# Delta rule: the next pair's squares, row sums and decay rows placed ahead of this pair's output norm and turn

## The chip, the cores and the metric

One core of a Trainium2 chip. The metric is the device time of one execution in microseconds; the kernel before takes 4389.96 us (median of 3 runs, 4386.17 to 4395.65).

## The reference, cut to what matters

The kernel is one inference step of a decoder layer: a projection, a gated delta rule beside sparse attention, an output projection and a convolutional feed-forward network, for 2048 prompt tokens and 8 sample tokens. The change touches the delta rule over the prompt (4 heads of 128, processed in chunks). For each chunk and head:

```python
q = l2_normalize(q) * (GDN_DK ** -0.5)      # needs the row sums of q*q
k = l2_normalize(k)                         # needs the row sums of k*k
gc = jnp.cumsum(g, axis=-1)
diff = gc[..., :, None] - gc[..., None, :]
decay = jnp.where(lower, jnp.exp(jnp.where(lower, diff, 0.0)), 0.0)
a_mat = jnp.where(strict, jnp.einsum('bhnid,bhnjd->bhnij', k * beta[..., None], k) * decay, 0.0)
sol = triangular_solve(a_mat + eye, [v * beta, k * beta * exp(gc)])
...
def step(s, xs):                            # from chunk to chunk
    v_new = u_c - w_c @ s
    o = q_c @ s + qk_c @ v_new
    s = s * gl_c + k_c.T @ v_new
    return s, o
...
o = rms_norm(o, out_gain) * jax.nn.silu(z)  # needs the row sums of o*o
```

## The kernel before, in words

`build` runs phases one after the other, each closed by a barrier: projection, channels, `heads`, mix, feed-forward up and down. `heads` has two parts. The second, named "mid", runs the delta rule (`Delta`) with attention heads of 8 query tiles (`Attention`, the tiles in `LATE`) beside it.

**Tiling.** The prompt is 16 chunks of 128 tokens, taken in 8 pairs `j`; `b` is 0 or 1 in a pair, `n = 2j + b`. Four heads lie side by side, so that most tiles are 128 x 512 fp32. Each chunk `b` has two PSUM tiles of one bank, `A[b]` and `B[b]`; the other four banks belong to the attention.

**Order.** Each engine has a written order of instructions (methods `tensor`, `scalar`, `gpsimd`, `vector`, `sync` of `Delta`), tied together by semaphores in `S`. In each pair, on TensorE: row sums of the squares (L1893, each matmul against ones, 64 columns); decay rows (L1902); key turn (L1908), value turn (L1915), normalised keys turned back (L1921), Gram products (L1930), system turned (L1937); six levels of the block inverse (L1949, L1957, L1959); then `W` (L1966), new values (L1975, L1976), state update product (L1981) and outputs (L1985, L1986), the last four chunk by chunk, since chunk 1 needs the state of chunk 0; last the normed outputs turned (L1996).

ScalarE squares q and k (L2009), takes exponentials of the decays (L2013, L2020, L2021), the root of the key and query sums (L2016), copies PSUM tiles out (L2027, L2033, L2039, L2045, L2050), squares the output (L2053), and takes the root for the output norm (L2056). VectorE reads the sums (L2121), forms the decay differences (L2128 to L2130), scales the keys (L2133, L2136), applies the decays (L2152, L2155), updates the inverse (L2164 to L2179), updates the state (L2188), reduces the output squares (L2194 to L2198), scales the output (L2201, L2203) and gates it (L2209). GpSimd spreads the gates (L2072), forms the two scaled keys (L2079, L2080), masks decays (L2085) and scales queries (L2087). SyncE loads q, k, v and z, and stores the result.

**Attention beside.** `Beside` is a generator of attention steps. After each piece of the delta rule an engine calls `side.spend(w)`, with a weight `W_...` of that piece. It issues attention steps until the share of the attention's total weight (248.0) that is issued reaches the share of the rule's total (833.6) that is spent, 0.2975 to 1. All engines spend the same weights in the same order, so each sees the same attention step at the same place. On TensorE a step is a score product (L1603 with L1605 or L1607), or four blocks turned (L1618) and the weighting of the blocks before (L1654). On ScalarE it is the eviction of a score (L1680) or of turned blocks (L1689), or a head's exponential (L1694), with square roots for the query norm at L1724. On VectorE it is a head's bias and maximum (L1770, L1771), for which the exponential waits.

Of the kernel before, what the change touches and what calls it, by code (L numbers as in the profile page):

```python
# [1456 lines left out]
class Attention:  # L1457
# [32 lines left out]
    def rows(self, t):  # L1490

        return slice(self.tiles[t] * P, self.tiles[t] * P + P)
# [309 lines left out]
class Delta:  # L1802
# [47 lines left out]
    def sync(self, sp, side, pairs, ahead):  # L1850
        S, N = self.S, self.N
        if 0 in pairs:
            sp.dma_start(self.gain[:, :], self.out_gain).then_inc(S["gain"], 16)
        for j in pairs:
            side.spend(2 * (self.W_SUMS + self.W_ROWS + self.W_TURN_K + self.W_TURN_V + self.W_BACK + self.W_GRAM))
            if j == 0:
                for b in range(2):
                    self.load_z(sp, b)
# [5 lines left out]
            for w in (self.W_SYS, *[self.W_YV + self.W_PROD] * (LEVELS - 1), self.W_WT, self.W_VNEW, self.W_KVO, self.W_NORM):  # L1864
                side.spend(2 * w)
            for b in range(2):
# [17 lines left out]
    def tensor(self, pe, side, pairs):  # L1884
        K, S, A, B = self.K, self.S, self.A, self.B
        for j in pairs:
            for b in range(2):
                n = j * 2 + b
                pe.wait_ge(S["sq"], n + 1)
                if j:  # L1890
                    pe.wait_ge(S["on"], n - 1)
                for i in range(2 * GH):
                    last = pe.matmul(self.sums_in(B[b])[:, i, :], self.kwd[b][:, i, :], K.ones[:, 0:64], start=True, stop=True)  # L1893
                last.then_inc(S["ss"], 1)
                side.spend(self.W_SUMS)
# [73 lines left out]
            for b in range(2):  # L1969
# [31 lines left out]
    def scalar(self, act, side, pairs):  # L2001
        S, A, B, st = self.S, self.A, self.B, self.st
        for j in pairs:
            for b in range(2):
# [5 lines left out]
                side.spend(self.W_SUMS)  # L2010
            for b in range(2):
                act.wait_ge(S["dif"], j * 2 + b + 1)
                act.activation(self.er[b][:, :, :], A[b][:, :, :], ACT.Exp).then_inc(S["er"], 1)  # L2013
                if b == 1:
                    act.wait_ge(S["sums"], j * 2 + 2)
                    act.activation(st[:, :, 8:12], st[:, :, 4:8], ACT.Sqrt).then_inc(S["root"], 1)  # L2016
                side.spend(self.W_ROWS)
            for b in range(2):
# [28 lines left out]
            for b in range(2):  # L2047
# [5 lines left out]
                act.activation(self.kwd[b][:, 0:GH, :], B[b][:, :, :], ACT.Square).then_inc(S["osq"], 1)  # L2053
# [1237 lines left out]
```

## Time and profile before

| | us |
|---|---|
| median of 3 runs | 4389.96 |
| the profiled execution's own time | 4385.17 |
| its span, first to last instruction | 4383.7 |
| TensorE busy in the span | 3860.7 (88%) |
| VectorE busy | 2198.2 (50%) |
| ScalarE busy | 1552.3 (35%) |
| GpSimd busy | 651.7 (15%) |
| mean granted TensorE clock | 0.928 |

The time of an execution is its span and a little around it (1.5 us here). The page and the views give busy times by engine, by stretch and by line; a line is that of the kernel's source. Idle time of an engine counts only where the engine sets the pace. The granted clock is 1 at 2.4 GHz and 0.5 at 1.2 GHz; a stretch's mean lies between.

### The profile page before, as it was taken

To read this page: it belongs to the slowest core of one execution; us is meant where nothing else is said; L and a number is where in the kernel's file an instruction comes from. 1 tells how busy PE (TensorE), PEld (TensorE's weight loads), DVE (VectorE), ACT (ScalarE), POOL (GpSimd) and SP (SyncE) were. 2 spreads that over 40 slices of the span, in tenths; PEclk is the share of its full clock that TensorE was granted. 3 is DMA by queue.
4 is the path that set the end of the run, shared out by engine and by line. 5 is a ranking of instruction groups with operands and counts; after the bars stand their busy time and mean duration, and the time that the engine had idled before them with its cause. 6 is when DMAs were issued, how large, how long until landed. Compare 5 with 4: busy or idle time off the path is not lost. (4 is left out here: it accounts for less than half of the span.)

```text
span 4383.7 us, 51967 instructions
## 1 busy us (share of the span) xinstructions
PE 3860.7 (88%) x19810; PEld 3155.5 (72%) x19882; DVE 2198.2 (50%) x4366; ACT 1552.3 (35%) x2462; POOL 651.7 (15%) x530
## 2 busy tenths in 40 slices
PE   7998887788859877888888779899999999979999
PEld 4554454455448556777777778799999999958787
DVE  6648988998953583343433343443444444330200
ACT  2135565565636333333433331322222222221211
POOL 0000000000000003222322220011111111024443
PEclk9998999999979677999988889999999999989999
DMA  3342212120141201111111114311211112064433
GB/s 111 96 97 62 67 41 78 37 65 25 54 172 64 68 12 56 28 35 34 32 33 33 44 51 129 102 39 39 58 39 47 49 39 58 29 206 135 130 117 109
DMA packets 287498, 298.52 MB, mean 68 GB/s; under 512 B 33871, under 2 KB 231375, under 8 KB 282410
## 3 DMA queue, kind: packets, MB, share of 16 engines
q1 hardware_dynamic: 264254, 249.46, 20.0%
q10 hardware_dynamic: 20944, 25.59, 1.7%
q0 software_dynamic: 2112, 20.97, 1.3%
q8 instruction: 117, 1.92, 0.2%
q14 instruction: 71, 0.58, 0.0%
HBM read 202.15 MB, written 94.10 MB: 68 GB/s over the span
## 5 line engine op out<-in xcount | busy, mean ns | idle before, releaser
L538 PE MATMUL chan_p_g<-ht,w_chan 128*128 128x412 f32 (+1 forms) x1760 | 677.3, 528 | 53.4 <-ACT chan_flat L586 33.7
L949 PE MATMUL up_p_g<-ht_high,up_wh 128*128 128x412 f32 (+1 forms) x1760 | 617.2, 351 | 0.2 <-POOL up_wl L1006 0.2
L949 PE MATMUL up_p_g<-ht_low,up_wh 128*128 128x412 f32 (+1 forms) x1760 | 615.3, 350 | 0.0
L949 PE MATMUL up_p_g<-ht_high,up_wl 128*128 128x412 f32 (+1 forms) x1760 | 615.0, 349 | 0.0
L538 PEld LDWEIGHTS chan_p_g<-ht,w_chan 128*128 128x128 f32 x1760 | 341.3, 197 | 300.6 <-issue 233.4
L970 ACT ACTIVATE up_pre<-up_p_g 128x412 f32<-128x412 f32 (+1 forms) x220 | 113.2, 515 | 738.1 <-PE up_p_g L949 738.1
L1348 ACT ACTIVATE chan_signed<-chan_sc,chan_trial 128x512 bf16<-128x512 f32 (+6 forms) x224 | 304.9, 1361 | 148.5 <-DVE chan_trial L1403 127.8
L1038 DVE TENSOR_SCALAR up_acc<-up_pre,up_taps 128x2048 f32<-128x2048 f32 x44 | 59.3, 1347 | 557.4 <-ACT up_pre L970 557.4
L949 PEld LDWEIGHTS up_p_g<-ht_high,up_wh 128*128 128x128 f32 x1760 | 331.5, 188 | 1.8 <-POOL up_wl L1006 0.6
L949 PEld LDWEIGHTS up_p_g<-ht_low,up_wh 128*128 128x128 f32 x1760 | 331.3, 188 | 1.2
L949 PEld LDWEIGHTS up_p_g<-ht_high,up_wl 128*128 128x128 f32 x1760 | 331.2, 188 | 0.5
L1389 DVE TENSOR_SCALAR_CACHE_REDUCE chan_tie<-chan_sc,chan_trial 128x384 bf16<-128x384 f32 (+6 forms) x224 | 316.3, 1412 | 7.6
L1006 POOL TENSOR_TENSOR up_wl<-up_w,up_wh 128x1024 fp32r<-128x1024 f32 x44 | 131.3, 2984 | 1085.3 <-ACT up_wh L964 826.5
L1324 PE MATMUL chan_p_sc<-ik,chan_iq 128*128 128x512 f32 (+3 forms) x304 | 187.0, 619 | 101.5 <-ACT chan_r L1343 91.1
L1206 PE MATMUL down_p_y<-down_wl,down_ah 128*128 128x512 f32 x704 | 274.4, 390 | 0.0
L1205 PE MATMUL down_p_y<-down_wh,down_ah 128*128 128x512 f32 x704 | 274.3, 390 | 0.0
L1207 PE MATMUL down_p_y<-down_wh,down_al 128*128 128x512 f32 x704 | 274.2, 389 | 0.0
L1177 POOL TENSOR_TENSOR down_al<-down_a,down_ah 128x1024 fp32r<-128x1024 f32 x88 | 211.8, 2406 | 356.9 <-ACT down_ah L1151 356.9
L1343 ACT ACTIVATE chan_r<-chan_p_sc 128x512 f32<-128x512 f32 (+3 forms) x304 | 159.6, 543 | 222.5 <-PE chan_p_sc L1325 116.2
L1151 ACT ACTIVATE down_ah<-down_a 128x1024 fp32r<-128x1024 f32 x88 | 93.3, 1060 | 382.3 <-PE down_p_y L1207 374.3
L1222 DVE TENSOR_TENSOR down_x<-down_p_y,down_x 128x512 f32<-128x512 f32 (+1 forms) x34 | 21.1, 680 | 388.0 <-PE down_p_y L1207 388.0
L1375 DVE SCALAR_TENSOR_TENSOR chan_sc<-chan_r,chan_iw,chan_sc 128x512 f32<-128x512 f32 (+3 forms) x266 | 172.6, 683 | 54.1 <-ACT chan_r L1343 51.7
(561 smaller groups left out, 7033.9 us busy)
## 6 DMA issues: line engine op xcount, KB each, us to landing
down_a<-scratch_act SPq DMA_DIRECT2D x88, 512.0 KB, 3.7
scratch_act<-up_acc SPq DMA_DIRECT2D x22, 1028.0 KB
up_w<-in_w_up SPq DMA_DIRECT2D x44, 512.0 KB, 6.4
chan_iq<-scratch_iq SPq DMA_DIRECT2D x28, 512.0 KB, 7.2
scratch_qkv<-chan_acc SPq DMA_DIRECT2D x12, 1028.0 KB, 4.6
keys_of_raw<-scratch_qkv SPq DMA_DIRECT2D x16, 768.0 KB, 5.4
w_chan<-in_w_in SPq DMA_DIRECT2D x22, 512.0 KB, 4.5
proj_x<-in_x_prompt SPq DMA_DIRECT2D x16, 512.0 KB, 3.9
```

The source lines that it names most:

```text
L538: last = pe.matmul(p_g[u % BANKS][:, 0:cols.stop - cols.start], weights[:, k, :], K.ht[:, k, cols], start=(k == 0), stop=(k == KD - 1))
L949: last = pe.matmul(p_g[u][:, 0:cols.stop - cols.start], wp[s][:, k, :], hp[:, k, cols], start=(k == 0 and m == 0), stop=(k == KD - 1 and m ...
L1006: pool.tensor_tensor(wl[s][:, :, :], w[s][:, :, :], wh[s][:, :, :].bitcast(F32), ALU.subtract).then_inc(s_wl[s], 1)
L1177: pool.tensor_tensor(al[t % RING][:, :, :], a[t % RING][:, :, :], ah[t % RING][:, :, :].bitcast(F32), ALU.subtract)\
L1205: pe.matmul(bank[0:m, :], hi, wh[:, f, :], start=(f == 0), stop=False)
L1206: pe.matmul(bank[0:m, :], hi, wl[:, f, :], start=False, stop=False)
L1207: last = pe.matmul(bank[0:m, :], lo, wh[:, f, :], start=False, stop=(f == NF - 1))
L1324: pe.matmul(out, self.iq[b][:, 0, h, :], self.K.ik2[:, cols], start=True, stop=False)
L1343: act.activation(self.r[n % self.RING][:, 0:width], self.p_sc[n % 2][:, 0:width], ACT.Relu).then_inc(S["relu"], 1)
L1348: act.activation(self.signed[:, 0:nk], self.sc[1][:, 0:nk], ACT.Sign, scale=-1.0, bias=self.trial[:, 1:2].bitcast(F32), accum_out=self.sig ...
L1375: dve.scalar_tensor_tensor(out=s[:, cols], in0=r, scalar=w, in1=s[:, cols], op0=ALU.mult, op1=ALU.add)\
L1389: last = dve.tensor_scalar(self.tie[:, 0:na], self.sc[0][:, 0:na], trial[:, 0:1].bitcast(F32), None, ALU.is_ge, ALU.add, accum_out=count[: ...
```

## The change

For pairs 1 to 7 the first three steps of a pair move ahead of the output norm, gate and turn of the pair before. To make room in PSUM, the sums go to `A[b]` instead of `B[b]`, the outputs are turned into `B[b]` instead of `A[b]`, and the output squares go to a free tile of the inverse (`y[1]`) instead of `kwd`, which then holds the next pair's squares. The waits follow. The root of the key and query sums now stands ahead of the exponentials and right behind the root of the output norm. The weights are spent in the new order on every engine.

```diff
@@ sync
+        side.spend(2 * (self.W_SUMS + self.W_ROWS))
+        for b in range(2):
+            self.load_z(sp, b)
         for j in pairs:
-            side.spend(2 * (self.W_SUMS + self.W_ROWS + self.W_TURN_K + self.W_TURN_V + self.W_BACK + self.W_GRAM))
-            if j == 0:
-                for b in range(2):
-                    self.load_z(sp, b)
+            side.spend(2 * (self.W_TURN_K + self.W_TURN_V + self.W_BACK + self.W_GRAM))
...
+            if j + 1 < N // 2:
+                side.spend(2 * (self.W_SUMS + self.W_ROWS))
+            side.spend(2 * self.W_NORM)
@@ tensor
-        for j in pairs:
+
+        def begin(j):
             for b in range(2):
                 n = j * 2 + b
                 pe.wait_ge(S["sq"], n + 1)
                 if j:
-                    pe.wait_ge(S["on"], n - 1)
+                    pe.wait_ge(S["state"], n - 1)
                 for i in range(2 * GH):
-                    last = pe.matmul(self.sums_in(B[b])[:, i, :], self.kwd[b][:, i, :], K.ones[:, 0:64], start=True, stop=True)
+                    last = pe.matmul(self.sums_in(A[b])[:, i, :], self.kwd[b][:, i, :], K.ones[:, 0:64], start=True, stop=True)
                 last.then_inc(S["ss"], 1)
                 side.spend(self.W_SUMS)
             for b in range(2):
                 n = j * 2 + b
                 pe.wait_ge(S["gb"], n + 1)
-                if j:
-                    pe.wait_ge(S["res"], n - 1)
+                pe.wait_ge(S["sums"], n + 1)
                 for h in range(GH):
                     last = pe.matmul(A[b][:, h, :], self.el[b][:, h, :], K.upto[:, :], start=True, stop=True)
                 last.then_inc(S["row"], 1)
                 side.spend(self.W_ROWS)
-            for b in range(2):
-                pe.wait_ge(S["sums"], j * 2 + b + 1)
+        begin(pairs[0])
+        for j in pairs:
+            for b in range(2):
+                if j:
+                    pe.wait_ge(S["res"], j * 2 + b - 1)
                 for h in range(GH):
                     last = pe.matmul(B[b][:, h, :], self.raw[b][:, GH + h, :], K.ident[:, :], start=True, stop=True)
                 last.then_inc(S["turnk"], 1)
@@ tensor, after the outputs
+            if j + 1 < self.N // 2:
+                begin(j + 1)
             side.spend(self.W_NORM)
             side.spend(self.W_NORM)
             for b in range(2):
                 n = j * 2 + b
                 pe.wait_ge(S["on"], n + 1)
-                pe.wait_ge(S["state"], n + 1)
                 for h in range(GH):
-                    last = pe.matmul(A[b][:, h, :], self.kn[b][:, h, :], K.ident[:, :], start=True, stop=True)
+                    last = pe.matmul(B[b][:, h, :], self.kn[b][:, h, :], K.ident[:, :], start=True, stop=True)
@@ scalar: begin(j), called as on TensorE, after the output squares
                 act.activation(self.kwd[b][:, :, :], self.raw[b][:, 0:2 * GH, :], ACT.Square).then_inc(S["sq"], 1)
                 side.spend(self.W_SUMS)
+            if j:
+                act.wait_ge(S["mean"], j)
+                act.activation(st[:, :, 20:24], st[:, :, 16:20], ACT.Sqrt).then_inc(S["oroot"], 1)
+            act.wait_ge(S["sums"], j * 2 + 2)
+            act.activation(st[:, :, 8:12], st[:, :, 4:8], ACT.Sqrt).then_inc(S["root"], 1)
             for b in range(2):
                 act.wait_ge(S["dif"], j * 2 + b + 1)
                 act.activation(self.er[b][:, :, :], A[b][:, :, :], ACT.Exp).then_inc(S["er"], 1)
-                if b == 1:
-                    act.wait_ge(S["sums"], j * 2 + 2)
-                    act.activation(st[:, :, 8:12], st[:, :, 4:8], ACT.Sqrt).then_inc(S["root"], 1)
                 side.spend(self.W_ROWS)
...
-                act.activation(self.kwd[b][:, 0:GH, :], B[b][:, :, :], ACT.Square).then_inc(S["osq"], 1)
+                act.activation(self.y[1][b][:, :, :], B[b][:, :, :], ACT.Square).then_inc(S["osq"], 1)
@@ gpsimd: begin(j) holds the copy of L2072 and its weights, called after the weights of KVO
@@ vector
+        def sums(j):
+            if j:
+                dve.wait_ge(S["mean"], j)
             for b in range(2):
                 dve.wait_ge(S["ss"], j * 2 + b + 1)
-                dve.tensor_scalar(st[:, b, 0:8], self.sums_in(B[b])[:, :, 0], EPS, None, ALU.add).then_inc(S["sums"], 1)
+                dve.tensor_scalar(st[:, b, 0:8], self.sums_in(A[b])[:, :, 0], EPS, None, ALU.add).then_inc(S["sums"], 1)
                 side.spend(self.W_SUMS)
+
+        def rows(j):
             for b in range(2):
                 n = j * 2 + b
                 dve.wait_ge(S["row"], n + 1)
...
             dve.tensor_tensor(st[:, :, 16:20], st[:, :, 16:20], st[:, :, 0:4], ALU.add).then_inc(S["mean"], 1)
-            side.spend(self.W_NORM)
+            if j + 1 < self.N // 2:
+                sums(j + 1)
             dve.wait_ge(S["oroot"], j + 1)
             step(dve.reciprocal(st[:, :, 16:20], st[:, :, 20:24]))
             for b in range(2):
                 dve.tensor_tensor(self.kn[b][:, :, :], B[b][:, :, :], self.col(st[:, b, 16:20]), ALU.mult).then_inc(S["on"], 1)
+            if j + 1 < self.N // 2:
+                rows(j + 1)
+            side.spend(self.W_NORM)
             side.spend(self.W_NORM)
```

## Rows read from the trace of the kernel before

**Rows 1.** Stretches, mid phase: window, its us, each engine's busy us (instructions), clock, DMA

```profile
1747.00:2612.00 865.00, 723.80 (x5208) 664.41 (x5248) 325.07 (x738) 313.70 (x551) 240.19 (x281) 0.91 0.12 33
```

**Rows 2.** Same view, columns as above: the seven stretches between pairs, and their sum

```profile
1849.20:1889.90 40.70, 30.46 (x214) 28.23 (x213) 22.09 (x48) 17.77 (x29) 12.36 (x12) 0.92 0.31 83
1947.70:1988.60 40.90, 29.08 (x167) 23.48 (x169) 22.09 (x48) 20.31 (x31) 13.96 (x13) 0.92 0.24 65
2059.40:2097.90 38.50, 28.06 (x219) 25.89 (x217) 22.15 (x48) 17.62 (x28) 12.27 (x12) 1.00 0.32 89
2156.50:2196.80 40.30, 31.42 (x183) 25.75 (x183) 22.08 (x48) 20.51 (x30) 13.64 (x13) 0.92 0.25 65
2261.30:2309.60 48.30, 34.07 (x216) 31.36 (x214) 21.94 (x48) 17.39 (x26) 10.48 (x10) 0.86 0.26 71
2370.90:2416.30 45.40, 35.04 (x185) 29.11 (x186) 22.09 (x48) 19.66 (x28) 10.49 (x10) 0.81 0.22 58
2488.60:2536.30 47.70, 34.35 (x222) 31.15 (x221) 23.33 (x51) 19.72 (x30) 12.20 (x12) 0.85 0.21 66
sum 301.80, PE 222.48 PEld 194.98 DVE 155.78 ACT 132.97 POOL 85.41; mean PE 31.78 PEld 27.85 DVE 22.25 ACT 19.00 POOL 12.20
```

**Rows 3.** Waits, 1745 to 2615: waiter <- releaser: us in total, times, longest

```profile
PE mid_p_A L1949 <- DVE mid_xt L2168: 36.9, 16, 6.1
...
PE mid_p_B L1893 <- ACT mid_kwd L2009: 29.3, 10, 5.7
...
PE mid_p_A L1996 <- DVE mid_kn L2203: 18.9, 7, 3.2
...
PE mid_p_A L1930 <- ACT keys_of_raw L2027: 10.0, 6, 2.8
```

**Rows 4.** Groups, ScalarE, same stretch: table loads, count, busy us and mean ns

```profile
L1724 ACT ACT_TABLE_LOAD x8 | 10.3, 1283 | 0.1
L2016 ACT ACT_TABLE_LOAD x8 | 10.3, 1283 | 0.1
...
L2056 ACT ACT_TABLE_LOAD x4 | 5.1, 1283 | 0.1
```

**Rows 5.** Order of time, 2045 to 2085: start, us, instruction, [idle before <- releaser]

```profile
2055.47 1.02 PE L1603 MATMUL mid_p_a_l<-keys_of_kt,mid_a_qg 128*128 128x512 f32 x2
...
2059.43 0.60 ACT L2053 ACTIVATE mid_kwd<-mid_p_B 128x512 f32<-128x512 f32 x1 [1.99 <-PE mid_p_B L1986]
...
2062.66 1.29 DVE L2203 TENSOR_TENSOR mid_kn<-mid_p_B,mid_st 128x512 f32<-128x512 f32 x2
...
2063.41 1.16 PE L1996 MATMUL mid_p_A<-ident,mid_kn 128*128 128x128 f32 x8 [2.69 <-DVE mid_kn L2203]
...
2064.60 0.75 DVE L2209 SCALAR_TENSOR_TENSOR mid_x<-mid_p_A,mid_gain,mid_z 128x512 f32<-128x512 f32 x1 [0.66 <-PE mid_p_A L1996]
...
2065.52 1.04 ACT L2009 ACTIVATE mid_kwd<-keys_of_raw 128x1024 f32<-128x1024 f32 x1
...
2066.62 2.00 PE L1893 MATMUL mid_p_B<-ones,mid_kwd 128*128 128x64 f32 x16 [0.61 <-ACT mid_kwd L2009]
...
2072.09 1.11 PE L1902 MATMUL mid_p_A<-upto,mid_el 128*128 128x128 f32 x8
...
2073.24 0.69 DVE L2128 TENSOR_TENSOR mid_et<-mid_p_A,gc 128x512 f32<-128x512 f32 x1 [0.78 <-PE mid_p_A L1902]
...
2073.97 0.43 DVE L2129 TENSOR_SCALAR mid_el<-mid_et 128x512 f32<-128x512 f32 x1
...
2081.19 0.20 DVE L2133 RECIPROCAL mid_st<-mid_st 128x8 f32<-128x8 f32 x1 [2.43 <-ACT mid_st L2016]
...
2083.20 1.04 POOL L2080 TENSOR_TENSOR mid_kwd<-mid_kn,kdec 128x512 f32<-128x512 f32 x1
```

**Rows 6.** Order of time, VectorE, 2371 to 2416: maximum of an attention head

```profile
2379.82 2.29 DVE L1771 TENSOR_REDUCE mid_a_bias<-mid_a_lg 128x1 f32<-128x2048 f32 x1
```

**Rows 7.** Order of time, ScalarE, same stretch: the exponential behind that maximum

```profile
2382.14 2.00 ACT L1694 ACTIVATE mid_a_lg<-mid_a_lg,mid_a_bias 128x2048 f32<-128x2048 f32 x1 [6.08 <-DVE mid_a_bias L1771]
```

More of the change, by code:

```diff
@@ L2002, in scalar, with begin @@
         S, A, B, st = self.S, self.A, self.B, self.st
-        for j in pairs:
+        def begin(j):
             for b in range(2):
@@ L2013, in scalar @@
                 act.activation(self.er[b][:, :, :], A[b][:, :, :], ACT.Exp).then_inc(S["er"], 1)
-                if b == 1:
-                    act.wait_ge(S["sums"], j * 2 + 2)
-                    act.activation(st[:, :, 8:12], st[:, :, 4:8], ACT.Sqrt).then_inc(S["root"], 1)
                 side.spend(self.W_ROWS)
+        begin(pairs[0])
+        for j in pairs:
             for b in range(2):
@@ L2052, in scalar @@
                 act.wait_ge(S["kvo"], n + 1)
-                act.activation(self.kwd[b][:, 0:GH, :], B[b][:, :, :], ACT.Square).then_inc(S["osq"], 1)
+                act.activation(self.y[1][b][:, :, :], B[b][:, :, :], ACT.Square).then_inc(S["osq"], 1)
                 side.spend(self.W_KVO)
-            act.wait_ge(S["mean"], j + 1)
-            act.activation(st[:, :, 20:24], st[:, :, 16:20], ACT.Sqrt).then_inc(S["oroot"], 1)
+            if j + 1 < self.N // 2:
+                begin(j + 1)
+            else:
+                act.wait_ge(S["mean"], j + 1)
+                act.activation(st[:, :, 20:24], st[:, :, 16:20], ACT.Sqrt).then_inc(S["oroot"], 1)
             side.spend(self.W_NORM)
@@ L2066, in gpsimd, with begin @@
             pool.memset(K.state[:, :, :], 0.0).then_inc(S["zero"], 1)
-        for j in pairs:
+        def begin(j):
             for b in range(2):
@@ L2075, in gpsimd @@
             side.spend(self.W_ROWS)
+        begin(pairs[0])
+        for j in pairs:
             for b in range(2):
@@ L2106, in gpsimd @@
                 side.spend(self.W_PROD)
-            for w in (self.W_WT, self.W_VNEW, self.W_KVO, self.W_NORM, self.W_OUT):
+            for w in (self.W_WT, self.W_VNEW, self.W_KVO):
+                side.spend(w)
+                side.spend(w)
+            if j + 1 < self.N // 2:
+                begin(j + 1)
+            for w in (self.W_NORM, self.W_OUT):
                 side.spend(w)
@@ L2131, in vector @@
                 side.spend(self.W_ROWS)
+        sums(pairs[0])
+        rows(pairs[0])
+        for j in pairs:
             dve.wait_ge(S["root"], j + 1)
@@ L2193, in vector @@
                 dve.wait_ge(S["osq"], j * 2 + b + 1)
-                last = dve.tensor_reduce(st[:, b, 16:20], self.kwd[b][:, 0:GH, :], AX.X, ALU.add)
+                last = dve.tensor_reduce(st[:, b, 16:20], self.y[1][b][:, :, :], AX.X, ALU.add)
             dve.tensor_scalar(st[:, :, 0:4], st[:, :, 0:4], EPS * HD, None, ALU.mult)
@@ L2208, in vector @@
                 dve.wait_ge(self.s_z[b], j * 16 + 16)
-                dve.scalar_tensor_tensor(out=self.x[b][:, :, :], in0=A[b][:, :, :], scalar=self.gain[:, 0:1], in1=self.z[b][:, :, :],
+                dve.scalar_tensor_tensor(out=self.x[b][:, :, :], in0=B[b][:, :, :], scalar=self.gain[:, 0:1], in1=self.z[b][:, :, :],
                                          op0=ALU.mult, op1=ALU.mult).then_inc(S["res"], 1)
```

5 lines of the change are left out of this document (3 added, 2 removed).

## The prediction, made before the changed kernel was run

> **What bounds the kernel now.** I read the busy time in stretches first. The delta rule's phase with its side attention fills 1747 to 2612 us [rows 1]. It is the only part that the diff touches; before and after it lie barriers, so what is saved there comes off the end whole. TensorE is busy 723.8 of these 865 us, no other engine over 326, and its clock is 0.91. So TensorE sets the pace, and a gain is idle time of TensorE or time at its low clock. Next I cut out the stretch from the last output matmul of one pair (L1986) to the first level matmul of the next (L1949), which I call a seam. There are seven, numbered 0 to 6 by the pair that ends [rows 2]. They last 301.8 us, with 222.5 busy, so 79.3 idle: 10.2, 11.8, 10.4, 8.9, 14.2, 10.4 and 13.4. Seam 2 alone has the full clock throughout, so its 28.06 us busy is what the work costs at full clock; 7 x 28.06 = 196.4, and the missing 26.1 us are the price of the low clock. A seam without idle and low clock would be 28 us; the seven average 43.1.
>
> Then I asked the list of waits what ends the idle [rows 3]. Three chains show. The output norm: TensorE waits for L2203 before it turns the outputs (18.9 us). The next pair's squares: it waits for L2009 (29.3 us in ten waits, the longest 5.7). The keys: L1930 waits 10.0 us for ScalarE. The wait of L1949 (36.9 us over all eight pairs) belongs to the first inverse step, which the change leaves alone. Last the activation tables: 39 loads in the phase, six groups between 8 and 4 each, 1.283 us apiece, three of them in [rows 4]. The list in order of time [rows 5] shows one seam as a chain: outputs scaled, turned, gated; only then the squares of the next pair.
>
> **The change, part by part.** Prices are per seam; all durations are from [rows 5] unless another group stands there.
>
> Removed, norm wait. The turn waited for the chain of reduce, root and scale (2.69 idle at L1996). Afterwards TensorE has the row sums (2.00 twice) and decay rows (1.11 twice) to do first, 6.2 us, and VectorE's chain behind the last sums (0.2 read, 0.2 reciprocal, 1.29 for both scalings) is 1.9 with latencies. The decay rows cover it. Price of this wait: nothing left.
>
> Left at the front. TensorE still has nothing until the first square: 0.60 for the output square L2053 (the size of the other full-tile evictions) and 1.04 for L2009, 1.65 us together. Seven times: 11.5 us. The second square stands in ScalarE's queue behind one attention step. By the kernel's own sharing rule (0.2975 side units for each main unit) that step is a score eviction in seams 0 and 4 and a transposed-block eviction in 2 and 6; in 1, 3, 5 none falls there. A score must first be made (L1603, 1.02), evicted (about 0.65), then 1.04 squared: TensorE idles about 1.8. After a transposed block it has a weighting of 1.0 to do: 0.65. Sum 2 x 1.8 + 2 x 0.65 = 4.9 us.
>
> Added, wait of the key turn (L1908) for the gated output (`res`). Behind it in TensorE's queue stand the value turn and everything else; nothing else of the pair can start. VectorE must take the second decay differences first (0.69 + 2 x 0.43 = 1.6), then gate (0.75). With two turns (L1996, 1.16 each, about 0.95 from start to start) and one side step on TensorE this is covered in seams 0 and 1. Where an attention maximum (L1770, L1771: 0.4 + 2.29, [rows 6]) falls into the chain, it isn't. The sharing rule puts it between the two gatings in seam 2, after the second differences in 3, 4 and 5, and between the differences in 6. VectorE is then free for gating 4.5 us after the second decay row (rows: 0.2 + 1.6 + 2.7), the gate is done at 5.35, and TensorE has 2.7 to 4.3 of work: idle 1.6, 1.1, 1.15; in seam 6 about 2.2, in seam 2 1.3. Sum 7.4 us. Bounds: 0, if side steps are longer than I count, and 4.9 a seam (34 us) if nothing covers the chain.
>
> Moved, key root. Both square roots now stand together, ahead of the exponentials, and the root of the key sums is ready before the decay rows. L2133 waited 2.43 for it behind two exponentials and a table load; that goes. The key scaling can follow the key turn at once, before the value turn, and about 3 us earlier against the rest. Counting the order of Exp and Sqrt on ScalarE, with the side steps, gives the 39 loads of the trace for the old order and 23 for the new. The 16 loads are 16 x 1.283 = 20.5 us of ScalarE, which is busy 313.7 of 865 us [rows 1]: alone worth nothing; they count where ScalarE delays kh (L2027) and with it L1930. There the maximum and exponential of the attention stay in the chain, so I keep all 10.0 us of L1930's wait [rows 3] as the remaining idle between key turn and Gram products. Bounds: 0 to 10.
>
> The Trainium skill (ScalarE: Activation LUTs, What ACT_TABLE_LOAD costs) puts a switch at 1283 ns plus a drain of 1380 ns. The load agrees; no drain stands in this trace, where a 2.43 us wait holds the load, the Sqrt and the end of an exponential; with a drain of that size it could not. By that page the root would come an estimated 1.38 us sooner still in each seam, 9.7 us in seven, and the sum would be 4336.
>
> Kept: L1949's first wait. 36.9 us over eight pairs [rows 3], 7/8 of it in the seams' pairs, half before the first chunk's matmul: 16.1 us.
>
> Without price: the swap of PSUM tiles A and B for sums and output turn, and the output squares into y[1], keep counts and shapes. TensorE's new wait for `state` before the sums ends with L2188's four operations right after L1986, within the 1.65. VectorE's wait for `mean` is for its own last small operation (at most 0.2, beside the sums). GpSimd's copy L2072 is early in either order. SyncE: gating comes 8 to 10 us later in the seam, so the stores and the loads of z do too; z is used one pair (about 100 us) later, and `ahead` is used after the phase. The z loads for pair 0 come earlier. Pair 0's root order: 0 to -1.3 us, taken as 0.
>
> Sum of idle after: 11.5 + 4.9 + 7.4 + 10.0 + 16.1 = 49.9, against 79.3: 29.4 saved.
>
> Clock. The loss of 26.1 us comes with idle: seams 0 to 3 (8.9 to 11.8 idle) were busy (30.46 + 29.08 + 28.06 + 31.42)/4 = 29.76, a loss of 1.7 each; seams 4 to 6 (10.4 to 14.2) were busy 34.07, 35.04 and 34.35, a loss of 6.4 each [rows 2]. In 4 to 6 an attention exponential that waits for VectorE (6.08 us, [rows 7]) stood before or between the squares. The new order has it behind them in every seam. So I take 1.7 for all seven: 11.9, 14.2 saved. Bounds: 0 and 26.1.
>
> Total 43.6 us. The profiled execution took 4385.2 (span 4383.7), so 4341.6; the median of the runs is 4.8 above it, so 4346.
>
> **The rivals.**
> *Clock stays.* The sums' 64-column matmuls stand together behind an idle front, and the seams, which hold these sums, have a clock of 0.81 to 0.92 but for one [rows 2]. Against it: the seams with short idle lose little. Then only the 29.4 come: 4361.
> *The next wait.* Keys are ready earlier, but GpSimd needs five operations of 1.04 from there to the first masked decay and three more for the second. I count 8.2 us against 10.7 of TensorE work. If the side steps there are short, 3 us a seam come back: 4346 + 21 = 4367.
> *Nothing comes.* TensorE's gaps only change place, because each fused step still waits for its partner; within 0.2% (about 9 us, what a measurement of this kernel can tell from no change): 4390.
> *Slower, by the order of VectorE's queue.* The output scaling now stands behind both sums, and gating behind both decay differences and a maximum. If TensorE's side steps cover none of it, each seam has 1.65 + 1.8 + 4.9 = 8.35 idle, 58.5 in all, with 26.1 kept: 84.6, above the 79.3 before, and with long idle in each seam all take the clock loss of seams 4 to 6 (7 x 6.4 = 44.8, 18.7 more): 4390 + 24 = 4414. It decides from 11.3 us idle a seam. Against it: by the sharing rule six of the seven seams have an attention step (L1603 is one, [rows 5]) between the last decay row and the last output turn.
> The Trainium skill (PSUM — Partial Sum Buffer, Engine vs sequencer instructions) says that the queues of ScalarE, VectorE and GpSimd are strictly first in, first out; by it this rival's 4414 is what an uncovered chain gives. The trace agrees: the squares L2009 waited behind an exponential.
>
> **How the numbers follow.** Forecast (4330 to 4358) 0.44, clock 0.23, next wait 0.18, nothing 0.08, slower 0.07. Faster by over 0.2% 0.85, the same 0.08, slower 0.07. Best case: idle terms three and four at 0 (17.4) and no clock loss (11.9): 4317; I cut at 4322. The upper end goes past the third case with 9 us of error, 4376; what lies outside is mostly the last two.
>
> **What would show it.** Right: seven seams of 36 to 38 us; 23 table loads; L1996 without a wait; no wait of L2133 for a root; waits of L1908 for L2209 of 1 to 2 us in seams 2 to 6; L1893's waits near 2 us each; clock in the seams 0.9 or more in all. Wrong: L1908 waiting 4 us or more (slower rival), L2152 waiting for L2085 (next wait), seams 4 to 6 still near 0.85 (clock), or a body between seams that grows by what the seam lost, which would mean that attention work was only shifted.

## The result, and the profile of the changed kernel

| | before | changed |
|---|---|---|
| median of the runs, us | 4392.6 (4386.2 to 4395.7, 4 runs) | 4343.7 (4343.0 to 4345.0, 4 runs) |
| profiled execution, own time / span | 4385.2 / 4383.7 | 4345.0 / 4343.6 |
| phase, first sums to last output matmul, us | 850.9 | 804.3 |
| ScalarE table loads in it | 39 | 23 |

The ratio is 0.9898, interval 0.9886 to 0.9910: faster by one per cent. 4346 had been forecast, in a range of 4322 to 4376. The ratio is worth some 45 us; the two profiled executions are 40.2 us apart.

The phase as one stretch, of the kernel before and then of the changed one. Columns: window, its us, busy us of TensorE, its weight loads, VectorE, ScalarE and GpSimd with their instructions, mean TensorE clock, DMA share, GB/s.

```profile
1748.50:2599.40 850.90, 718.94 (x5182) 659.92 (x5223) 318.97 (x722) 309.96 (x546) 239.11 (x279) 0.91 0.12 33
```

```profile
1754.80:2559.10 804.30, 715.09 (x5222) 651.83 (x5223) 319.27 (x722) 289.13 (x530) 240.50 (x279) 0.92 0.13 35
```

The phase is 46.6 us shorter. It started 6.3 us later in this profile, which is work ahead of it that the change does not touch, and 46.6 less 6.3 is the 40 us between the two spans. In further profiles the phase begins anywhere from 1735 to 1756 us. So below I compare the length of the phase and of the seams, not spans.

The seven seams of the changed kernel and their sum, same columns; they answer to [rows 2]:

```profile
1853.30:1888.30 35.00, 28.57 (x214) 26.74 (x214) 21.80 (x48) 14.88 (x27) 12.35 (x12) 0.95 0.35 97
1945.50:1982.00 36.50, 30.58 (x170) 24.53 (x168) 21.98 (x48) 17.52 (x29) 13.95 (x13) 0.86 0.27 73
2051.50:2089.30 37.80, 32.33 (x218) 30.52 (x219) 22.19 (x48) 15.17 (x26) 12.27 (x12) 0.86 0.33 90
2149.40:2188.30 38.90, 32.27 (x184) 26.05 (x182) 22.31 (x48) 18.39 (x28) 13.82 (x13) 0.87 0.26 68
2251.70:2287.10 35.40, 28.75 (x216) 25.80 (x216) 21.79 (x48) 14.61 (x24) 10.48 (x10) 1.00 0.33 90
2348.00:2384.10 36.10, 31.70 (x190) 25.91 (x188) 22.07 (x48) 17.31 (x26) 10.48 (x10) 0.91 0.28 74
2458.00:2496.60 38.60, 32.05 (x222) 29.47 (x223) 23.02 (x51) 16.93 (x28) 12.22 (x12) 0.91 0.26 82
sum 258.30, PE 216.26 PEld 189.01 DVE 155.16 ACT 114.81 POOL 85.57; mean PE 30.89 PEld 27.00 DVE 22.17 ACT 16.40 POOL 12.22
```

The seams fell from 301.8 to 258.3 us, by 43.5 of the phase's 46.6. The stretches between them stayed (510.1 us before, 508.6 after), so no attention work was pushed out into them. Idle in the seams is length less TensorE busy: 79.3 before, 258.3 - 216.3 = 42.0 now. Busy fell by 6.2. This profile holds 5222 matmul records in the phase where that of the kernel before holds 5182, and both hold 5223 weight loads. Busy time that a missing record leaves out counts as idle here, so the split of the gain into idle and busy is known to some 3 us only. The clock has two levels, 1.2 and 2.4 GHz, so a seam of length L at mean clock c spent 2 x (1 - c) x L at the lower one. For seam 1 that is 2 x 0.14 x 36.5 = 10.2 us. Summed from the clock's own records it is 65.1 us before and 47.8 after.

The waits of the changed kernel from 1750 to 2570 us (waiter, releaser, us in total, times, longest), answering to [rows 3]:

```profile
PE mid_p_A L1955 <- DVE mid_xt L2199: 34.8, 16, 6.1
PE mid_p_A L1897 <- ACT mid_kwd L2017: 22.3, 11, 5.5
...
PE mid_p_B L1914 <- DVE mid_x L2244: 8.2, 5, 3.1
...
PE mid_p_A L1936 <- ACT keys_of_raw L2039: 4.7, 3, 1.9
```

L1955 is the old L1949 (first level matmul), L1897 the old L1893 (sums), L1914 the old L1908 (key turn), L1936 the old L1930 (Gram product). The output turn, L1996 before and L2003 now, is gone from the list: its 18.9 us are gone, and the key turn has 8.2 instead. Two waits of the kernel before that stand in no list so far are gone too: those of an attention step (L1618) and of the turned-back keys (L1921), here from 1793 to 2615 us:

```profile
PE mid_p_a_t L1618 <- ACT mid_a_pt L1689: 8.2, 4, 3.9
...
PE mid_p_B L1921 <- DVE mid_kn L2136: 6.4, 5, 1.7
```

ScalarE's table loads and VectorE's reciprocal of the key root (count, busy us and mean ns, idle before), answering to [rows 4] and to L2133 in [rows 5]:

```profile
L1724 ACT ACT_TABLE_LOAD x8 | 10.3, 1283 | 0.1
L2026 ACT ACT_TABLE_LOAD x8 | 10.3, 1283 | 0.1
...
L1694 ACT ACT_TABLE_LOAD x3 | 3.8, 1283 | 0.1
L2021 ACT ACT_TABLE_LOAD x3 | 3.8, 1283 | 0.1
...
L2071 ACT ACT_TABLE_LOAD x1 | 1.3, 1283 | 0.0
```

```profile
L2164 DVE RECIPROCAL mid_st<-mid_st 128x8 f32<-128x8 f32 x8 | 1.5, 193 | 0.0
```

8 + 8 + 3 + 3 + 1 = 23 loads, and no idle ahead of the reciprocal, where 2.43 us stood in the seam of [rows 5].

The key turn's wait, in order of time, in seam 3 (start, us, instruction, idle before):

```profile
2165.00 0.43 DVE L1770 TENSOR_TENSOR mid_a_lg<-mid_a_lg,near 128x256 f32<-128x256 f32 x1 [1.13 <-ACT mid_a_lg L1680]
2165.46 2.15 DVE L1771 TENSOR_REDUCE mid_a_bias<-mid_a_lg 128x1 f32<-128x1920 f32 x1
2167.53 1.40 DVE L2244 SCALAR_TENSOR_TENSOR mid_x<-mid_p_B,mid_gain,mid_z 128x512 f32<-128x512 f32 x2
```

VectorE takes an attention maximum ahead of the gating. The output turn (L2003) had run from 2163.30 to 2165.25, so TensorE waited 3.1 us for the first gated output.

### The profile page after: what moved, and what is told of

Read it like the earlier page. It is cut to its first block and busy times, and to the rows that moved or that the text cites. A ratio compares the mean times of both kernels' runs of the same rounds, so it can differ in the third digit from the quotient of the medians.

```text
span 4343.6 us, 52016 instructions
## 1 busy us (share of the span) xinstructions
PE 3868.5 (89%) x19882; PEld 3152.5 (73%) x19882; DVE 2196.6 (51%) x4366; ACT 1532.5 (35%) x2446; POOL 653.1 (15%) x530
```

## The experiments

Times are medians. Each ratio is to runs of the kernel before made beside that kernel on the same chip, and their median was 4388.8 us for again to rows_late, 4379.0 for squares_early to max_late and 4389.6 for the last three. So kernels of different groups are compared by ratio, and not by median. "Idle" is seam length less TensorE busy, "low" the seams' time at the lower clock.

| kernel | seams | idle | low | phase | loads | median | ratio (95%) |
|---|---|---|---|---|---|---|---|
| before | 301.8 | 79.3 | 65.1 | 850.9 | 39 | 4392.6 | 1 |
| changed | 258.3 | 42.0 | 47.8 | 804.3 | 23 | 4343.7 | 0.9898 (0.9886, 0.9910) |
| again | 258.7 | 44.7 | 47.8 | 803.6 | 23 | 4339.9 | 0.9897 (0.9865, 0.9929) |
| root_alone | 284.2 | 62.9 | 68.3 | 829.3 | 29 | 4365.3 | 0.9945 (0.9929, 0.9960) |
| root_late | 265.8 | 47.7 | 58.0 | 814.0 | 39 | 4348.8 | 0.9912 (0.9885, 0.9938) |
| rows_late | 253.6 | 44.7 | 37.5 | 797.9 | 23 | 4330.8 | 0.9879 (0.9851, 0.9907) |
| squares_early | 223.4 | 28.9 | 10.2 | 770.5 | 23 | 4297.1 | 0.9815 (0.9799, 0.9831) |
| sums_wide | 239.9 | 45.5 | 3.4 | 782.2 | 23 | 4310.9 | 0.9846 (0.9830, 0.9863) |
| sums_thin | 265.0 | 44.2 | 64.9 | 812.8 | 23 | 4338.3 | 0.9904 (0.9888, 0.9921) |
| max_late | 262.9 | 50.0 | 44.4 | 805.2 | 23 | 4332.9 | 0.9897 (0.9881, 0.9914) |
| before_wide | 294.2 | 76.6 | 61.4 | 843.0 | 39 | 4374.6 | 0.9971 (0.9957, 0.9984) |
| early_wide | 222.4 | 29.0 | 6.8 | 767.7 | 23 | 4301.2 | 0.9807 (0.9792, 0.9822) |
| early_wide_rows | 220.2 | 28.5 | 3.4 | 766.1 | 23 | 4301.8 | 0.9805 (0.9792, 0.9819) |

### again: the changed kernel once more

> The changed kernel itself, once more, beside the others of this group: 4343 to 4346 us.

Measured 4339.9 (4334.2 to 4351.2), ratio 0.9897. Seams, phase and the sum at the low clock are those of the first profile, but spread differently: seam 2 was at 0.86 above and at 1.00 here, seam 0 at 0.95 above and at 0.86 here.

```profile
1849.10:1886.50 37.40, 30.58 (x213) 28.45 (x214) 21.84 (x48) 14.89 (x27) 12.36 (x12) 0.86 0.33 90
...
2050.30:2084.20 33.90, 27.54 (x219) 25.95 (x218) 21.90 (x48) 15.18 (x26) 12.29 (x12) 1.00 0.37 101
```

So the clock of a single seam is not a property of its order of work alone. Only sums over seven seams are compared from here on. This profile holds 5182 matmul records, as that of the kernel before does, and it has 44.7 us of idle and 214.0 of busy time. Of each kernel one execution is profiled, which can lie up to 7 us from the kernel's median (max_late's took 4326.1, its median is 4332.9), so differences of a few us between seams are weak evidence.

### root_alone and root_late: what is the key root worth?

root_alone is the kernel before with the key root moved, and nothing else:

```
+            act.wait_ge(S["sums"], j * 2 + 2)
+            act.activation(st[:, :, 8:12], st[:, :, 4:8], ACT.Sqrt).then_inc(S["root"], 1)
             for b in range(2):
                 act.wait_ge(S["dif"], j * 2 + b + 1)
                 act.activation(self.er[b][:, :, :], A[b][:, :, :], ACT.Exp).then_inc(S["er"], 1)
-                if b == 1:
-                    act.wait_ge(S["sums"], j * 2 + 2)
-                    act.activation(st[:, :, 8:12], st[:, :, 4:8], ACT.Sqrt).then_inc(S["root"], 1)
```

> The kernel before, with one edit: the root of the key and query sums stands ahead of the two exponentials instead of behind them. Theory A (several causes: norm wait, key root, waits for squares, clock): only the idle before the key turn-back and the Gram products goes, which was 18.5 us in the seven seams; 8 to 12 us of it, so 4380 to 4385 with 23 table loads. Rival B (the order of the roots, with the table loads, is what brought the gain): 4345 to 4350.

root_late is the changed kernel with the same lines put back behind the second exponential.

> The changed kernel, with the root of the key sums back behind the two exponentials. Theory A: 8 to 12 us given back, 4352 to 4356, idle again before the key turn-back. Rival B: nearly everything given back, 4385 or more.

The sum of the seven seams, root_alone and then root_late:

```profile
sum 284.20, PE 221.26 PEld 194.57 DVE 155.70 ACT 122.39 POOL 85.36; mean PE 31.61 PEld 27.80 DVE 22.24 ACT 17.48 POOL 12.19
```

```profile
sum 265.80, PE 218.08 PEld 191.60 DVE 155.35 ACT 132.99 POOL 85.57; mean PE 31.15 PEld 27.37 DVE 22.19 ACT 19.00 POOL 12.22
```

Alone, the root takes 17.6 us off the seams and some 24 off the time. Of the 17.6, 16.4 are idle (79.3 to 62.9); TensorE's busy time hardly moves (222.5 to 221.3). Taken out of the changed kernel it costs 7.5 us of seams; the medians are 9 us apart, with intervals that overlap. That is what theory A had, and rival B fell. The two do not add: 17.6 on one side, 7.5 on the other. The waits in the seams show where the 16.4 us of idle were: with the root moved alone, L1618's fell from 8.2 to 0.7 us, L1921's from 6.4 to 0.4 and L1930's from 6.3 to 4.1. In root_late the first two stay away (0.8 and none), so there the rest of the new order keeps them covered. So root_alone fell between the expectations, with the gain in idle larger than I had it. I had also expected 23 loads in root_alone and 29 were there. The pairing of the two roots in one table needs both moves; 10 of the 16 saved loads come with the root's own move.

root_late has 39 loads, 16 more than the changed kernel, or 20.5 us of ScalarE (133.0 us busy in the seams against 114.8), and is only 7.5 us longer there. The table loads are not what the time is made of; the wait behind them is.

### rows_late: need the decay rows move?

The changed kernel, with the decay rows (TensorE), their differences (VectorE) and exponentials (ScalarE) called at the top of each pair, behind the output turn and the gating:

```
+        def decay(j):
             for b in range(2):
                 n = j * 2 + b
                 pe.wait_ge(S["gb"], n + 1)
...
         begin(pairs[0])
         for j in pairs:
+            decay(j)
```

> The changed kernel, but with only squares and row sums ahead of the output norm; decay rows, their differences and exponentials stand behind the output turn as before. Theory A: TensorE reaches the output turn right after the second sums and waits for VectorE's read, reciprocal and first scaling, about 1.3 to 2 us a seam, and decay rows no longer cover it: 4353 to 4358. Rival C (the squares alone are the gain, and the decay rows only change place): 4343 to 4346.

```profile
sum 253.60, PE 208.89 PEld 182.89 DVE 153.74 ACT 114.61 POOL 85.34; mean PE 29.84 PEld 26.13 DVE 21.96 ACT 16.37 POOL 12.19
```

Both expectations missed: it is the faster kernel in the profile, seams 253.6 against 258.3 and 258.7, phase 797.9 against 804.3 and 803.6, median 4330.8. The ratios (0.9879 and 0.9897) have intervals that overlap, so the gain stands on the phase of one profile. What the runs show is no gain from moving the rows. I had thought that the decay rows must cover the norm chain ahead of the output turn. They need not: that turn waits at most 0.5 us in any seam here. Behind the output turn they cover something else. The gating no longer stands behind the second differences, and TensorE has the two decay groups to do while it is made, so the key turn no longer waits for it (8.2 us before). Two other waits come instead, of the value turn (L1924) and of an attention step:

```profile
PE mid_p_a_t L1618 <- ACT mid_a_pt L1689: 3.9, 2, 2.0
PE mid_p_A L1924 <- ACT mid_er L2031: 3.7, 3, 1.9
```

Idle is as before (44.7, as in the changed kernel's second profile); the seams are shorter by the busy time, 208.9 against 216.3 and 214.0. So of the three things that the change moves ahead, the decay rows are the one whose move no run shows to be worth anything.

### squares_early: the idle at the front

In the changed kernel ScalarE still squares the next pair's queries and keys only after the last output matmul, into a tile that the products of the state update have to free. Here it does so earlier, into two tiles that are free by then:

```
+        def squares(j, b):
+            act.wait_ge(self.s_raw[b], j * 16 + 16)
+            act.activation(self.x[b][:, :, :], self.raw[b][:, 0:GH, :], ACT.Square)
+            act.activation(self.y[0][b][:, :, :], self.raw[b][:, GH:2 * GH, :], ACT.Square).then_inc(S["sq"], 1)
...
+            if j + 1 < self.N // 2:
+                squares(j + 1, 0)
             for b in range(2):
                 act.wait_ge(S["vnew"], n + 1)
                 act.activation(self.at[b][:, :, :], B[b][:, :, :], ACT.Copy).then_inc(S["vnc"], 1)
+                if b == 0 and j + 1 < self.N // 2:
+                    squares(j + 1, 1)
```

> The changed kernel, with the next pair's squares taken by ScalarE before this pair's outputs are made, into two free tiles, so that the row sums can start at once. Theory A: the idle ahead of and between the sums (1.6 to 3.4 us a seam, 14.9 in the seven) goes, and part of the low clock behind it: seams 10 to 20 us shorter in all, about 4325 to 4332 where the changed kernel takes 4340 to 4344. Rival D (idle ahead of the sums is only passed on to the wait of the key turn for the gated outputs, since VectorE's chain starts with the output squares all the same): 0 to 5 us, the key turn's wait grows from 8 to about 20 us.

```profile
sum 223.40, PE 194.53 PEld 172.12 DVE 154.26 ACT 101.78 POOL 85.64; mean PE 27.79 PEld 24.59 DVE 22.04 ACT 14.54 POOL 12.23
```

In order of time in seam 4, the last outputs and the first sums:

```profile
2211.01 0.39 PE L1992 MATMUL mid_p_B<-mid_at,mid_et 128*128 128x128 f32 x2
2211.13 0.97 PEld L1897 LDWEIGHTS mid_p_A<-ones,mid_x 128*128 128x128 f32 x8
2211.24 1.00 PE L1897 MATMUL mid_p_A<-ones,mid_x 128*128 128x64 f32 x8
```

and its waits, of 1750 to 2530 us:

```profile
PE mid_p_B L1914 <- DVE mid_x L2250: 7.7, 5, 3.2
...
PE mid_p_A L1936 <- ACT keys_of_raw L2041: 4.9, 3, 1.9
```

No wait stands between outputs and sums in any seam; the 7.9 us that L1897 still waits are all at the head of the phase. The seams are 34.9 us shorter than in the changed kernel: 13.1 of idle, and 21.7 of busy, from 216.3 to 194.5 (15.8 and 19.5 against the second profile of the changed kernel). The latter is what I had not expected in that size: with the same 64-column sums, the time at the low clock went from 47.8 to 10.2 us when the pause ahead of them went. The rival, that the key turn would wait for what the front gave up, fell: its 8.2 us are 7.7. The ratio is 0.9815, 1.85% under before and 0.83% under the changed kernel's, or 36 us; the phase is 33.8 us shorter. In its profile the phase also begins 20 us earlier (1734.8), and that part I do not put down to the edit.

### sums_wide, sums_thin, before_wide: why is the clock low?

The row sums are 16 matmuls a pair against a block of ones, 64 columns wide where one is needed. The trace has each of them as two instructions, so x16 is the eight matmuls of one chunk. In seam 2 of the changed kernel they ran so (order of time, TensorE):

```profile
2053.12 2.00 PE L1897 MATMUL mid_p_A<-ones,mid_kwd 128*128 128x64 f32 x16 [1.63 <-ACT mid_kwd L2017]
...
2057.19 3.68 PE L1897 MATMUL mid_p_A<-ones,mid_kwd 128*128 128x64 f32 x16
```

The first sixteen take 2.00 us, the second 3.68, though no idle stands ahead of them and their weight loads waited only 0.22 us. The record of the clock falls at 2055.45: 2.3 us after the pause of 1.63 us has ended and 0.3 us after the first sums. So the three kernels change the columns of these matmuls and nothing else: 128 columns on the changed kernel, 16 columns on it, and 128 columns on the kernel before. The last matmul of each eight keeps 64 in the wide form, where its tile ends.

```
-                    last = pe.matmul(self.sums_in(A[b])[:, i, :], self.kwd[b][:, i, :], K.ones[:, 0:64], ...)
+                    last = pe.matmul(A[b][...][:, i * 64:min(i * 64 + 128, 512)], self.kwd[b][:, i, :],
+                                     K.ones[:, 0:min(128, 512 - i * 64)], ...)
```

> The changed kernel, with the row-sum matmuls 128 columns wide instead of 64 (each next one overwrites the surplus). Theory E (the low clock in the seams comes with the thin matmuls of the sums): the low clock behind them goes in most seams, 47.8 us of low time down to under 20 and 10 us gained. Rival F (it comes with the idle front before them): low time as it is, and 0 to 6 us lost for the added columns.

> The changed kernel, with the row-sum matmuls 16 columns wide instead of 64. Theory E: more low clock in the seams, 60 to 80 us instead of 47.8, 5 to 15 us lost. Rival F: low time as it is, same time within 3 us.

> The kernel before, with the row-sum matmuls 128 columns wide. Theory E (the thin sums cause the low clock in the seams, in the old order too): low clock of the seams from 65.1 us to under 25, idle as it was (79), seams about 280 to 285 us instead of 301.7, and 16 to 22 us gained in all. Then the part of the change's gain that came from the clock was not bought by its shorter idle. Rival H (in the old order the long idle ahead of the sums is enough to bring the low clock): 45 us or more of low time stay, under 10 us gained.

Seams 1, 2 and 3 of sums_wide, and the sum of its seven:

```profile
1923.50:1955.80 32.30, 25.67 (x168) 20.89 (x169) 21.86 (x48) 17.54 (x29) 13.96 (x13) 1.00 0.30 82
2025.90:2059.80 33.90, 27.54 (x218) 25.97 (x219) 21.91 (x48) 15.18 (x26) 12.29 (x12) 1.00 0.37 101
2118.40:2152.60 34.20, 27.32 (x182) 22.40 (x183) 22.18 (x48) 18.18 (x28) 13.83 (x13) 1.00 0.30 78
...
sum 239.90, PE 194.39 PEld 170.94 DVE 154.18 ACT 114.62 POOL 85.65; mean PE 27.77 PEld 24.42 DVE 22.03 ACT 16.38 POOL 12.24
```

sums_thin, and then before_wide:

```profile
sum 265.00, PE 220.84 PEld 194.59 DVE 155.32 ACT 114.85 POOL 85.58; mean PE 31.55 PEld 27.80 DVE 22.19 ACT 16.41 POOL 12.23
```

```profile
sum 294.20, PE 217.57 PEld 190.09 DVE 155.57 ACT 133.06 POOL 85.68; mean PE 31.08 PEld 27.16 DVE 22.23 ACT 19.01 POOL 12.24
```

At the same idle (42.0 and 44.7; 45.5; 44.2) the low clock is 47.8 us with 64 columns, 3.4 with 128 and 64.9 with 16, and TensorE is busy 216.3, 194.4 and 220.8 us. The wide sums take 18.4 us off the seams, all of it busy time (21.9 us, and idle rose by 3.5; against the second profile 19.6 and 0.8). With the kernel before's 79 us of idle they do not help much: low 61.4 against 65.1, seams 7.6 us shorter, and a ratio of 0.9971, some 13 us with an interval of 7 to 19. The low clock stays as rival H had it; its gain of under 10 us is neither met nor excluded. In these kernels, then, long pauses kept the clock low with wide sums too, and short pauses kept it low only with narrow ones. Taking away either was enough: the pause ahead of the sums in squares_early, the narrow sums in sums_wide. Both gains are clear of the noise (ratios 0.9815 and 0.9846 against 0.9898). squares_early also has the least idle of the three, 28.9 us, so where a pause stands and how much idle there is in all are not told apart by it.

That fewer columns make it worse rests on one profile. sums_thin's ratio (0.9904) can't be told from the changed kernel's, which is what rival F had for the time, and its profiled execution was the slowest of its four (4344.2 us against 4337.5 to 4338.6).

### max_late: the key turn's wait

The key turn waits for the gating, and the gating stands behind an attention maximum in VectorE's queue. Here VectorE's attention steps of the seam all stand behind the gating:

```
             if j + 1 < self.N // 2:
                 rows(j + 1)
-            side.spend(self.W_NORM)
-            side.spend(self.W_NORM)
...
+            if j + 1 < self.N // 2:
+                side.spend(2 * (self.W_ROWS + self.W_NORM + self.W_OUT))
```

> The changed kernel, with VectorE's attention steps of the seam moved behind the gating, on VectorE alone. Theory A: the key turn's wait for the gated outputs (8.2 us in five of the seven seams, 3.1 and 2.5 in the largest) is the attention maximum ahead of the gating; it goes, 5 to 10 us gained in the seams. Rival G (the maximum is only late elsewhere: ScalarE's exponential waits for it and holds up the decay exponentials and turned blocks): the same idle reappears ahead of value turn, key turn-back or Gram products, no gain or a loss of up to 10 us.

```profile
sum 262.90, PE 212.90 PEld 186.87 DVE 154.41 ACT 113.47 POOL 85.57; mean PE 30.41 PEld 26.70 DVE 22.06 ACT 16.21 POOL 12.22
```

In order of time in seam 6, VectorE, ScalarE and TensorE:

```profile
2451.27 2.29 DVE L1771 TENSOR_REDUCE mid_a_bias<-mid_a_lg 128x1 f32<-128x2048 f32 x1
2453.59 2.00 ACT L1694 ACTIVATE mid_a_lg<-mid_a_lg,mid_a_bias 128x2048 f32<-128x2048 f32 x1 [5.72 <-DVE mid_a_bias L1771]
...
2457.28 1.12 PE L1618 MATMUL mid_p_a_t<-ident,mid_a_lg 128*128 128x128 f32 x4 [5.17 <-ACT mid_a_pt L1689]
```

The key turn does not wait at all. Yet idle rose to 50.0 and the seams to 262.9. The late maximum holds the exponential L1694, which stands at the head of ScalarE's queue with the block eviction L1689 behind it, and TensorE's next transposition of attention (L1618) waits 5.2 us for that. The Trainium skill (PSUM — Partial Sum Buffer, Engine vs sequencer instructions) says that ScalarE, VectorE and GpSimd take their queues strictly first in, first out; this trace agrees, with the 5.72 us at L1694. The wait was moved, not removed: with one order for each engine, the maximum has to stand somewhere. The phase (805.2) equals the changed kernel's.

### early_wide and early_wide_rows: put together

squares_early with the wide sums, and that with the late decay rows.

> The changed kernel with early squares and with wide sums. Theory: the two cures share the low clock of the sums; early squares left 10.2 us low and 29.0 us idle in the seams of 223.4 us. Together 217 to 221 us of seams, 3 to 8 us less than with early squares alone. Rival I (the gains of 35 and 18 us add up): seams near 205 us.

> The same with the decay rows behind the output turn again. Theory: the key turn no longer waits behind VectorE's decay differences and the attention maximum (8.9 us in the seams with early squares), but the value turn then waits for the exponentials of the decays (5.9 us when the rows stood there without the other two edits): 214 to 219 us of seams, 1 to 5 us less than early_wide. Rival J (with the sums done early nothing but the decay rows is left to cover VectorE's chain to the output turn, so TensorE waits there 1 to 2 us a seam): 5 to 12 us more than early_wide.

```profile
sum 222.40, PE 193.42 PEld 171.06 DVE 154.25 ACT 101.81 POOL 85.73; mean PE 27.63 PEld 24.44 DVE 22.04 ACT 14.54 POOL 12.25
```

```profile
sum 220.20, PE 191.67 PEld 169.50 DVE 153.70 ACT 101.63 POOL 85.48; mean PE 27.38 PEld 24.21 DVE 21.96 ACT 14.52 POOL 12.21
```

On the changed kernel the wide sums were worth 18.4 us of seams, on squares_early 1.0. They are two cures of the same loss. Rival I (205 us) and rival J fell; both seam lengths lie just over 1 us above what the theories gave. The key turn's wait with early squares, 8.9 us in the expectation, is 7.7 in the list of squares_early, and the value turn's 5.9 is 3.7 in that of rows_late. The three kernels with early squares have ratios of 0.9815, 0.9807 and 0.9805, which can't be told apart; each beats the changed kernel by 0.8 to 0.9% going by these ratios, and by 34 to 38 us going by the phase. Of the 28.5 us of idle left, 13.8 are the wait that ends each seam, of the first level for VectorE. It was 13.8 us in the seams of the kernel before too, and no kernel here moved it.

## Why the prediction was right, point by point

*What bounds the kernel.* TensorE's idle and its low clock in the seams were the place. 43.5 of the 46.6 us came out of the seams; 1.6 came from the head of the phase and 1.5 from the stretches between.

*The total.* 43.6 us predicted, 43.5 measured in the seams. The match is partly luck. Idle gave 37.3 (79.3 to 42.0) where I had 29.4, and the clock gave 6.2 (busy 222.5 to 216.3) where I had 14.2. Two misses of 8 us cancel. By the second profile of the changed kernel they are 34.6 and 8.5, and two misses of 5 to 6 us cancel.

*Idle, term by term,* in us of seven seams:

| term | predicted | measured |
|---|---|---|
| output turn's wait | 0 | 0, L2003 is not in the list of waits |
| front and second square | 11.5 + 4.9 = 16.4 | 14.9: 3.4, 1.7, 1.6, 1.7, 3.2, 1.7, 1.6 |
| key turn's wait for the gated output | 7.4 | 8.2 |
| Gram product's wait for ScalarE | 10.0 | 3.2 |
| first level's first wait | 16.1 | 13.8 (in the kernel before 13.8 too): 1.8, 2.4, 2.5, 1.7, 1.8, 1.2, 2.4 |
| other waits (L1654, L1943) | 0 | 2.1 |

Three of the five priced terms hold to 1.5 us, and the first level's is 2.3 off: less than half of L1949's 36.9 us stood before the first chunk's matmul. The front is 1.6 to 1.7 in five seams, as its 1.65 had it. The long ones are 0 and 4, where I had put an attention score between the squares; in 2 and 6 the exposed 0.65 did not come. The key turn waits 1.0, 3.1, 0.2, 1.5 and 2.5 us in seams 2 to 6; I had 1.3, 1.6, 1.1, 1.15 and 2.2, with seam 3's maximum behind the differences where it also is in the trace, but with less on TensorE to cover it. rows_late shows that this wait is the order of VectorE's queue, and max_late that it cannot be had away by moving the maximum alone.

The step that failed is the fourth: "I keep all 10.0 us of L1930's wait [rows 3] as the remaining idle between key turn and Gram products." In size it was wrong twice. Of these 10.0 us, 3.7 lay at the head of the phase, before the first pair, and not in a seam; the list by window would have shown it. Of the other 6.3, half went: 4.7 are left in the phase, 1.5 of them at the head, so 3.2 in the seams. I had argued that maximum and exponential stay in the chain. The wait is 6.3 us in the seams of the kernel before, 4.1 in root_alone, 4.2 in rows_late and 3.2 in the changed kernel. So the root alone takes 2.2 of it. Yet it is 2.6 in root_late, so the root's move is not needed for it once the rest stands; what the rest does here stays open.

A second step went unnamed. The sum compares 49.9 us with all of the 79.3, and so takes every other wait of the kernel before as gone. Two of these are large: 8.2 us of L1618 for the attention's turned blocks, a wait that the working never mentions, and 6.4 of L1921, which falls under "the key scaling can follow the key turn at once". Both did go, and root_alone shows that the root's move is enough for it. These 14.6 us are right in the sum, the first 8.2 of them without a reason.

*The clock.* The direction held, the reason did not, and the term is mis-sized: 14.2 us forecast, 6.2 and 8.5 measured. I had taken that the attention exponential ahead of the squares in seams 4 to 6 made their clock low, and that all seams would come to the level of 0 to 3. Seams 4 to 6 did recover: 1.00, 0.91 and 0.91, against 0.86, 0.81 and 0.85 [rows 2]. But seams 1 to 3, which have no such exponential and lost 2.3 to 5.9 us of idle each, got worse: 0.86, 0.86 and 0.87 against 0.92, 1.00 and 0.92 (0.86, 1.00 and 0.83 in the second profile, still 23.9 us at the lower clock where the three had 13.6). The loss after is 216.3 - 196.4 = 19.9 us, not 11.9. The 196.4 is itself a little high: sums_wide, at full clock but for 3.4 us, was busy 194.4. sums_wide and squares_early show that pause and narrow sums make the low clock of the new order together (low 3.4 and 10.2 against 47.8). Why this took more from seams 1 to 3 than in the old order, where the sums also had a wait ahead of them, no run shows. My rival "Clock stays" named these 64-column matmuls and dismissed them because seams with short idle had lost little, which was true of the old order only. The outcome lies between the forecast and that rival.

*The table loads.* 39 to 23, as counted. root_late holds all 39 and costs 7.5 us of seams: a load is worth something where a wait stands behind it. On the switch itself: the Trainium skill (ScalarE: Activation LUTs, What ACT_TABLE_LOAD costs) adds a drain of 1380 ns to each load of 1283 ns. The load agrees, the drain does not. In seam 3 the squares end at 2153.11, the load starts at 2153.13, and the Sqrt behind it at 2154.42:

```profile
2151.12 1.99 ACT L2017 ACTIVATE mid_kwd<-keys_of_raw 128x1024 f32<-128x1024 f32 x2
...
2153.13 1.28 ACT L2021 ACT_TABLE_LOAD   x1
...
2154.42 0.21 ACT L2021 ACTIVATE mid_st<-mid_st 128x8 f32<-128x8 f32 x1
```

So no drain of that size stands ahead of the load or behind it. The estimate made from it (4336) was 8 us too low against 4343.7.

*The rivals.* Next wait: L2152 waited 5.4 us for GpSimd's L2085 in the phase before; the changed kernel's list of VectorE's waits has no such entry, and the first level's wait (34.8, was 36.9) did not grow, so nothing moved to GpSimd. Nothing comes: ruled out by the ratio's interval. Slower by VectorE's queue: its mechanism is there, 8.2 us of it, but it needed 11.3 us of idle a seam and the seams have 42.0 / 7 = 6.0.

*Signs promised.* 23 loads, no wait of the output turn and none of VectorE for the key root: right. Seams of 36 to 38 us: 35.0 to 38.9, mean 36.9. L1914's waits of 1 to 2 us: 0.2 to 3.1. The sums' waits near 2 us: five of 1.6 to 1.7, two of 3.2 and 3.4. Clock of 0.9 or more in all: no, three are at 0.86 or 0.87 (in the second profile three are at 0.83 or 0.86). No growth between seams: right.

## What to carry to other kernels

When a pipeline is folded at its seam, write down for each engine which operation of its queue the next fused step waits for, and check it by window: a total over the phase hides what belongs to the head. Look at what is done ahead of the moved steps as well. The gain left at the front (35 us for early squares) was four fifths of the whole change's in the seams, and one of the moved parts (the decay rows) brought nothing that these runs can show. Name every wait that the old sum holds, too: two that the working did not price, 14.6 us together, were over a third of the idle that went.

## What the runs showed of the hardware that I had not expected

Sixteen instructions of the sums took 2.00 us at the full clock with 64 columns and 2.00 us with 128 (sums_wide, 1833.84 and 1838.69), and 1.96 with 16 columns (sums_thin, 1847.19). Their weight loads took 1.86 us in all three, so columns taken away save almost nothing.

They can cost something instead: with the idle of the seams nearly the same, the low clock was 47.8 us at 64 columns in two profiles and 3.4 at 128 in one (64.9 at 16, which the medians do not bear out). At 77 us of idle the wide sums left 61.4. I did not expect that a matmul that does more for the same time could give back 20 us of clock. What the chip looks at to decide this, these runs do not show.
